# Sample preparation inside the last projection tiles: memory values four requests at a time, rows spread by transfers, retention state updated without TensorE

## The chip, the cores and the metric

One core of one Trainium2 chip. TensorE multiplies (PE; its weight loads are PEld), VectorE is DVE, ScalarE is ACT, GpSimd is POOL, and SyncE (SP) only issues transfers (DMA). The metric is the time of one execution in microseconds on the device; for a timed kernel the median of several runs. All arithmetic is float32 or its TensorE form fp32r.

## The reference

One step of a decoder layer, for a prompt of 2048 tokens and for 8 sample requests of one token each. Every row is normalised and multiplied by one input projection; then three branches run side by side: retention (a recurrent state of 128x128 in each of 4 heads), latent attention over a paged cache of 16384 tokens per request, and cross attention over 256 memory keys and values. What this change touches is the sample side of retention and memory attention, and the head norm of the prompt's retention:

```python
def step(S, inp):                                   # retention, one chunk (a sample has one token)
    qb, kb, vb = inp
    sc = jnp.einsum('bihd,bjhd->bhij', qb, kb) * intra[None]
    o = (jnp.einsum('bhij,bjhe->bihe', sc, vb)
         + jnp.einsum('bihd,bhde->bihe', qb * q_dec[None, :, :, None], S))
    S = S * s_dec[None, :, None, None] + jnp.einsum('bjhd,bjhe->bhde', kb * k_dec[None, :, :, None], vb)
    return S, o

def head_norm(o, g):
    mu = jnp.mean(of, axis=-1, keepdims=True)
    var = jnp.mean((of - mu) ** 2, axis=-1, keepdims=True)
    y = ((of - mu) * lax.rsqrt(var + EPS)).reshape(B, T, H * dv)
    return (y * g.astype(jnp.float32)).astype(o.dtype)

def mem_attend(q, mk, mv):
    s = jnp.einsum('bthd,bmhd->bhtm', q, mk).astype(jnp.float32) * MEM_SCALE
    p = jax.nn.softmax(s, axis=-1).astype(mv.dtype)
    return jnp.einsum('bhtm,bmhd->bthd', p, mv).reshape(B, T, MEM_W)
```

## The kernel before

The kernel runs in stages, each in a block of its own with a barrier behind it. Two of them matter here.

**The projection** (up to about 917 us). The weight columns are cut into stripes, a stripe into tiles. A tile of the last stripes is 24 matmuls of 128x512 (`tile`, L675), into one of two banks of `pj_ps`: even tiles are read out by ACT (L473), odd ones by DVE (L571), and tile n can begin when tile n-2 has been read out. SP stores each pair of tiles to `s_zt` (L381). DVE and ACT also split each stripe's weights into high and low parts (L456, L539), and POOL loads the next stripe (L306). The last 24 tiles carry a second program, `SamplePrepare`: behind tile k each engine runs its own method with that k (`sample.tensor(k)`, `sample.vector(k)`, `sample.scalar(k)`, `sample.sync(k)`; POOL has four parts j = 0 to 3, the last beginning after its last weight load). I call what stands behind tile k "step k". Each engine goes through tiles and steps in program order, so a wait in a step also holds the tiles behind it on that engine. What the steps compute that the change touches:

- `spread(b)` (L2867), steps 4 to 11: one matmul each, which copies the memory query of request b to all 128 partitions; DVE multiplies the request's keys with it and sums (`memory_scores`, L2669 and L2672).
- `key_of(b)` on ACT and `outer(b)` on PE (L2856), steps 7, 8, 11, 12: the outer product of key and value of request b, four matmuls; DVE adds it to the decayed state (`new_state`, L2660). The state of four requests is loaded at a time (`load_state`), multiplied with the retention query (`retention`, L2875) and stored (`store_state`, POOL, j = 3).
- `memory_values(b)` (L2887), steps 14 to 21: eight matmuls of 128x32 weights with 128 columns, all of one request and so all into the same 32 partitions of the bank; two buffers for the loads of the values.
- the transposes of `w_uk` (L2911) and of the page table (L2914) in step 1.

**The sample attention with the prompt's retention** (about 922 to 1477 us). 64 steps g. POOL gathers a group of pages into one of four buffers, after the step that used the buffer is through (`pv_ps`); DVE turns it in three pieces (L2038), PE multiplies with it (L2262, L2275, L2286). Between these steps one block of 128 prompt rows is begun every four: its retention ends in step 4b+4 with `new_state`, `head_statistics` and `head_roots` on DVE, then `normalise` on ACT and `turn_retention` on PE. `head_roots` is `inverse_root` (L102 to L107, eleven small instructions in a chain) and one more (L2101).

Of the kernel before, what the change touches and what calls it, by code (L numbers as in the profile page):

```python
# [28 lines left out]
P = 128  # L29
# [1844 lines left out]
def sample_attention_and_retention(nc, t, keep):  # L1874
# [7 lines left out]
    with ExitStack() as ctx:  # L1882
# [49 lines left out]
        tmp = m.sb("tmp", [P, HEADS])  # L1932
# [14 lines left out]
         bias_ok, exp_ok_m, scT_ok, inv_ok, pn_ok, state_ok, root_ok, pT_ok, cat_m_ok, normed_ok, cat_r_ok, state_out) = [  # L1947
            m.sem(n) for n in ("consts qT_ps kT_ps mem_ps st_ps sc_ps out_ps pT_ps pv_ps rT_ps qT_ok kT_ok "
                               "bias_ok exp_ok scT_ok inv_ok pn_ok state_ok root_ok pT_ok cat_m_ok normed_ok cat_r_ok "
# [12 lines left out]
        with nc.Block() as block:  # L1962
# [48 lines left out]
            @block.gpsimd  # L2011
            def _(pool):
                for g in range(1, STEPS):
                    if g == 3:
                        pool.wait_ge(z_in[0], 32)
                    if g >= DEEP:
                        pool.wait_ge(pv_ps, g - DEEP + 1)
                    gather(pool, t, index, g, nat[g % DEEP], kp[g % DEEP], nat_in[g % DEEP])

            @block.vector  # L2020
            def _(dve):
# [66 lines left out]
                def head_statistics(b):  # L2088
                    for h in range(HEADS):
# [5 lines left out]
                    link(dve.tensor_scalar(var[:, :], mean_var[:, :, 1], EPS, None, ALU.add))  # L2095

                def head_roots(b):
                    if b >= 1:
                        dve.wait_ge(normed_ok, b)
                    inverse_root(dve, link, var[:, :], root[:, :], tmp[:, :])  # L2100
                    dve.scalar_tensor_tensor(shift[:, :], mean_var[:, :, 0], -1.0, root[:, :], ALU.mult, ALU.mult)\  # L2101
                       .then_inc(root_ok, 1)

                for g in range(STEPS + 2):
# [19 lines left out]
                    if begun(g, 3) is not None:  # L2124
                        head_roots(begun(g, 3))
# [310 lines left out]
class SamplePrepare:  # L2436


    def __init__(self, nc, t, ctx, r, keep, rows4, out_rows, banks, turned_over, banks_free, rows_out, gates_out):
        def sb(name, shape, dt=F32):  # L2440
# [8 lines left out]
        self.mem = ring[:, :].rearrange("p (j m n) -> p j m n", j=2, m=MT)  # L2449
# [36 lines left out]
        self.k_only = self.zq[:, 0:2 * W3].rearrange("b (j n) -> b j n", j=2)  # L2486
# [20 lines left out]
        (self.z_in, self.zq_in, self.rot_in, self.ident_in, self.small, self.pick_in, self.uq_in, self.uk_in, self.row_in, self.st_in,  # L2507
         self.zeros, self.chain, self.cqn_ok, self.kv_ok, self.qk_ok, self.q_ok, self.prod_ok, self.low_ok, self.st_ok, self.rg_ok,
         self.kq_ok, self.sm_ok, self.bias_ok, self.pm_ok, self.cq_ps, self.uk_ps, self.uq_ps, self.new_ps, self.qT_ps, self.ql_ps,
         self.qlT_ps, self.rq_ps, self.low_ps, self.outer_ps, self.ret_ps, self.retT_ps, self.rt_ps, self.rgT_ps, self.bc_ps,  # L2510
         self.smT_ps, self.pmT_ps, self.mo_ps, self.moT_ps, self.cqT_ok, self.ukT_ok, self.newT_ok, self.qnT_ok, self.ql_ok, self.q4_ok,
         self.rq_ok, self.ko_ok, self.rows_ok, self.ret_ok, self.exp_ok, self.pmp_ok, self.cats_ok, self.pages_in, self.pages_ok,
         self.index_ps, self.q_clear, self.queries_in, self.q32_ok, self.ret_out, self.out) = [r.sem("s_" + n) for n in (
            "z_in zq_in rot_in ident_in small pick_in uq_in uk_in row_in st_in "
            "zeros chain cqn_ok kv_ok qk_ok q_ok prod_ok low_ok st_ok rg_ok "
            "kq_ok sm_ok bias_ok pm_ok cq_ps uk_ps uq_ps new_ps qT_ps ql_ps "
            "qlT_ps rq_ps low_ps outer_ps ret_ps retT_ps rt_ps rgT_ps bc_ps "
            "smT_ps pmT_ps mo_ps moT_ps cqT_ok ukT_ok newT_ok qnT_ok ql_ok q4_ok "
            "rq_ok ko_ok rows_ok ret_ok exp_ok pmp_ok cats_ok pages_in pages_ok "
            "index_ps q_clear queries_in q32_ok ret_out out").split()]  # L2520
        self.mem_in = [r.sem(f"s_mem_in{j}") for j in range(2)]
# [6 lines left out]
    def sync(self, k, sp):  # L2528
        t, keep = self.t, self.keep

        def load_memory(name, b):
            sp.dma_start(self.mem[:, b % 2, :, :], self.memory_of(name, b)).then_inc(self.mem_in[b % 2], 16)
# [6 lines left out]
        if k == -1:  # L2539
# [14 lines left out]
            sp.dma_start(self.zq[:, :], t["s_zs"][:, 0:3 * W3]).then_inc(self.zq_in, 16)  # L2554
            sp.dma_start(self.zm[:, :], t["s_zs"][:, O_MQ:O_GATE]).then_inc(self.zq_in, 16)
# [15 lines left out]
        if k == 2:  # L2571
            sp.wait_ge(self.uq_ps, 1)
            load_state(0)
        if 4 <= k <= 9:
            sp.wait_ge(self.kq_ok, k - 3)
            load_memory("cache_mem_k", k - 2)
# [7 lines left out]
        if k == 9:  # L2584
# [3 lines left out]
        if k == 10:  # L2588
            sp.wait_ge(self.kq_ok, 7)
            load_memory("cache_mem_v", 0)  # L2590
        if k == 11:
            sp.wait_ge(self.kq_ok, 8)
            load_memory("cache_mem_v", 1)
        if 14 <= k <= 19:
            sp.wait_ge(self.mo_ps, k - 13)
            load_memory("cache_mem_v", k - 12)
# [40 lines left out]
    def vector(self, k, dve):  # L2637
# [17 lines left out]
        def new_state(b):  # L2655
            if b % HALF == 0:
                dve.wait_ge(self.st_in, 16 * (b // HALF + 1))
            dve.wait_ge(self.outer_ps, b + 1)
            for h in range(HEADS):
                last = dve.scalar_tensor_tensor(self.state[:, b % HALF, h, :], self.state[:, b % HALF, h, :], self.decay[h],  # L2660
                                                (A, B)[b % 2][:, h * HD:(h + 1) * HD], ALU.mult, ALU.add)
            last.then_inc(self.st_ok, 1)

        def memory_scores(b):
            if b == 0:
                dve.wait_ge(self.ql_ps, 1)
            dve.wait_ge(self.mem_in[b % 2], 16 * (b // 2 + 1))
            dve.wait_ge(self.bc_ps, b + 1)
# [410 lines left out]
```

## Time and profile before

| | |
|---|---|
| median of 3 runs | 2280.73 us (2277.04 to 2282.85) |
| the profiled execution's own time | 2287.12 us |
| its span, first to last instruction | 2285.4 us |
| PE busy, share of the span | 2135.5 us, 93% |
| DVE busy | 1293.5 us, 57% |
| ACT busy | 666.0 us, 29% |
| POOL busy | 230.3 us, 10% |
| granted TensorE clock, mean | 0.973 |

The profiled execution took 6.4 us more than the median of the timed runs, so differences are taken within the profile and then applied to the median. The times in the rows are microseconds from the start of the span. Busy shares say little by themselves: in each stage one has to see which engine waits, and what its wait ends on.

### The profile page before, as it was taken

The numbers are of one execution on the slowest core, as the hardware profiler recorded it, in microseconds if no ns is written. First come the engines' busy times: TensorE is split into PE (matmuls) and PEld (weight loads), VectorE is DVE, ScalarE is ACT, GpSimd is POOL, SyncE is SP. The second block draws the span as 40 slices with busy tenths as digits, with TensorE's granted clock in tenths as the row PEclk, the third lists the DMA queues.
The fourth block names the chain that finished last, engine by engine and source line by source line (L and its number), as shares of the span: only waits on it lengthen the run. The fifth ranks groups of instructions, "written<-read, shape, count | busy, mean of one in ns | idle before, by whom it ended". The sixth has DMA issues, their size and how long they took to land. (4 is left out here: it accounts for less than half of the span.)

```text
span 2285.4 us, 48464 instructions
## 1 busy us (share of the span) xinstructions
PE 2135.5 (93%) x20401; PEld 1791.2 (78%) x20401; DVE 1293.5 (57%) x2743; ACT 666.0 (29%) x1484; POOL 230.3 (10%) x295
## 2 busy tenths in 40 slices
PE   7999999999999999698999989869899999989998
PEld 6999999997777778476777767648788888768886
DVE  4412444111122431699899999767577777745555
ACT  5311222000111110143343333334345445521110
POOL 1000000000001000121222222011212110000000
PEclk9999999999999999799999999969999999999999
DMA  7322332211224542899999999488997282154542
GB/s 255 112 76 78 100 100 93 84 57 65 84 84 149 190 141 84 326 370 347 338 379 368 362 363 377 180 269 302 345 200 141 53 141 98 58 185 138 163 158 83
DMA packets 186972, 428.19 MB, mean 187 GB/s; under 512 B 15424, under 2 KB 104672, under 8 KB 178576
## 3 DMA queue, kind: packets, MB, share of 16 engines
q0 software_dynamic: 46640, 240.85, 32.2%
q1 hardware_dynamic: 140128, 184.41, 24.3%
q8 instruction: 154, 2.52, 0.4%
q14 instruction: 50, 0.41, 0.1%
HBM read 331.72 MB, written 93.30 MB: 186 GB/s over the span
## 5 line engine op out<-in xcount | busy, mean ns | idle before, releaser
L678 PE MATMUL pj_ps<-pj_wh,pj_xh 128*128 128x256 f32 (+1 forms) x1152 | 324.7, 282 | 2.8 <-issue 2.8
L678 PE MATMUL pj_ps<-pj_wh,pj_xl 128*128 128x256 f32 (+1 forms) x1152 | 322.2, 280 | 0.0
L678 PE MATMUL pj_ps<-pj_wl,pj_xh 128*128 128x256 f32 (+1 forms) x1152 | 322.1, 280 | 0.0
L571 DVE TENSOR_SCALAR pj_stage<-pj_ps 128x256 f32<-128x256 f32 (+2 forms) x72 | 38.5, 535 | 449.4 <-PE pj_ps L675 282.3
L678 PEld LDWEIGHTS pj_ps<-pj_wh,pj_xh 128*128 128x128 f32 x1152 | 218.7, 190 | 10.6 <-issue 10.1
L2038 DVE STREAM_TRANSPOSE sa_turned<-sa_nat 128x2048 f32<-128x2048 f32 x96 | 220.0, 2291 | 10.4 <-DMA sa_kp<-cache_kpe,keep_index 10.4
L2262 PE MATMUL sa_ps_s<-sa_turned,keep_q 128*32 128x128 f32 x5120 | 183.1, 278 | 38.4 <-DVE sa_turned L2038 34.6
L678 PEld LDWEIGHTS pj_ps<-pj_wl,pj_xh 128*128 128x128 f32 x1152 | 218.8, 190 | 0.0
L678 PEld LDWEIGHTS pj_ps<-pj_wh,pj_xl 128*128 128x128 f32 x1152 | 218.7, 190 | 0.0
L675 PE MATMUL pj_ps<-pj_xh,pj_wh 128*128 128x512 f32 x512 | 208.2, 407 | 0.0
L675 PE MATMUL pj_ps<-pj_xl,pj_wh 128*128 128x512 f32 x512 | 204.1, 399 | 0.0
L675 PE MATMUL pj_ps<-pj_xh,pj_wl 128*128 128x512 f32 x512 | 203.6, 398 | 0.0
L2262 PEld LDWEIGHTS sa_ps_s<-sa_turned,keep_q 128*32 128x32 f32 x5120 | 135.2, 111 | 64.7 <-DVE sa_turned L2038 43.0
L473 ACT ACTIVATE pj_stage<-pj_ps 128x256 f32<-128x256 f32 (+2 forms) x72 | 34.1, 473 | 426.4 <-PE pj_ps L675 249.2
L1429 DVE TENSOR_TENSOR la_pl<-la_ps_p,la_ph 128x512 fp32r<-128x512 f32 (+1 forms) x144 | 88.4, 656 | 72.0 <-ACT la_ph L1475 72.0
L675 PEld LDWEIGHTS pj_ps<-pj_xh,pj_wh 128*128 128x128 f32 x512 | 97.9, 191 | 33.8 <-issue 12.4
L675 PEld LDWEIGHTS pj_ps<-pj_xl,pj_wh 128*128 128x128 f32 x512 | 97.6, 191 | 22.6
L675 PEld LDWEIGHTS pj_ps<-pj_xh,pj_wl 128*128 128x128 f32 x512 | 98.2, 192 | 21.2
L1466 ACT ACTIVATE la_row<-la_row,la_soft 128x128 f32<-128x128 f32 (+7 forms) x64 | 77.2, 1206 | 128.2 <-DVE la_soft L1416 128.2
L2286 PE MATMUL sa_ps_o<-sa_nat,sa_p_turned 128*16 128x256 f32 x1536 | 97.5, 385 | 9.8 <-issue 9.7
L1408 DVE CUSTOM_DVE_ANT_0 la_row<-la_ps_s,begin_causal 128x512 f32<-128x512 f32 (+3 forms) x160 | 92.2, 605 | 9.9 <-PE la_ps_s L1532 9.9
L1475 ACT CAST la_ph<-la_ps_p 128x512 fp32r<-128x512 f32 (+1 forms) x144 | 74.4, 565 | 39.3 <-PE la_ps_p L1545 38.4
(455 smaller groups left out, 4324.8 us busy)
## 6 DMA issues: line engine op xcount, KB each, us to landing
pj_raw<-w_in POOLq DMA_DIRECT2D x22, 1024.0 KB, 6.1
s_zn<-pj_stage SPq DMA_DIRECT2D x64, 256.0 KB, 2.2
s_zt<-pj_stage SPq DMA_DIRECT2D x32, 512.0 KB, 2.7
rm_z<-s_zn SPq DMA_DIRECT2D x16, 768.0 KB
pn_x<-x_prompt SPq DMA_DIRECT2D x16, 512.0 KB, 3.7
s_k<-lp_st SPq DMA_DIRECT2D x16, 512.0 KB, 8.8
s_v<-lp_st SPq DMA_DIRECT2D x32, 256.0 KB, 4.6
s_qn<-lp_st SPq DMA_DIRECT2D x16, 512.0 KB, 5.4
```

Source lines behind the costliest of these rows:

```text
L473: act.activation(stage_view(n, w_tile), ps[:, bank_of(n), 0:w_tile], ACT.Copy, scale=factor(s)).then_inc(ev_act, 1)
L571: dve.tensor_scalar(stage_view(n, w_tile), ps[:, bank_of(n), 0:w_tile], factor(s), None, ALU.mult).then_inc(ev_dve, 1)
L675: mm = pe.matmul(ps[:, bank_of(n), :], wt[:, k, m * P:(m + 1) * P], of[c // 2][:, k, c % 2 * 512:(c % 2 + 1) * 512], **flags)
L678: mm = pe.matmul(ps[:, bank_of(n), 0:w], of[u // 8][:, k, u % 8 * P:(u % 8 + 1) * P], wt[:, k, 0:w], **flags)
L1408: dve.tensor_tensor_reduce(out=row[:, s, q, c * P:(c + w) * P], in0=ps_s[:, (at + n) % 3, 0:w * P], in1=m, scale=1.0, scalar=-3.0e38, op0= ...
L1429: dve.tensor_tensor(pl[:, n % RING, 0:w], ps_p[:, n % RING, 0:w], ph[:, n % RING, 0:w], ALU.subtract).then_inc(pl_ok, 1)
L1466: act.activation(row[:, s, q, 0:n], row[:, s, q, 0:n], ACT.Exp, bias=soft[:, s, q, 1:2], scale=MLA_SCALE, accum_out=soft[:, s, q, 2:3]).th ...
L1475: act.copy(ph[:, n % RING, 0:w], ps_p[:, n % RING, 0:w]).then_inc(ph_ok, 1)
L2038: dve.transpose(turned[:, s, a:z, :, :].rearrange("p c x q -> p x c q"), of.rearrange("p x (c q) -> p x c q", q=QR)).then_inc(t_ok, 1)
L2262: mm = pe.matmul(ps_s[j * QR:(j + 1) * QR, s, 0:TQ * QR], q32[:, u, c, :], turned[:, s, c, j * TQ:(j + 1) * TQ, :].rearrange("p x q -> p ( ...
L2286: mm = pe.matmul(ps_o[j * QR:j * QR + ROWS_Q, 0:KVL], p_turned[:, s, x, j, :], nat[g % DEEP][:, TQ * j + x, :], start=(x == 0), stop=(x == ...
```

## The change

What it does, part by part:

- **Memory queries** are copied to 128 partitions by a transfer for each request (`query_row`, in `load_keys`) in place of `spread`.
- **State**: ACT multiplies the loaded state of four requests by the decay (`fade_state`, steps 4 and 9); `new_state` takes the key as a column of scalars from four more small transposes in step 3 (`keys`), and the value from a row copied to 128 partitions by a transfer (`value_row`, loaded in steps -1, 5, 6 and 10). `key_of` and `outer` are gone. `new_state` moves to steps 5, 6, 10, 11, `retention` to steps 7 and 12.
- **Memory values**: four value buffers (two in `ring`, two in the place of the state), `memory_values(i)` for four requests in steps 15 and 18, the requests in the innermost loop.
- **Order**: the transposes of `w_uk` and pages go from step 1 to step 2, behind the products with `w_uq`; the steps behind follow.
- **Head roots** of the prompt's retention go from DVE to POOL, by a power.

```diff
+                def head_roots(b):
+                    pool.wait_ge(power_ok, 1 + 2 * b)
+                    pool.wait_ge(var_ok, b + 1)
+                    if b >= 1:
+                        pool.wait_ge(normed_ok, b)
+                    pool.tensor_tensor(root[:, :], var[:, :], half[:, :], ALU.pow).then_inc(power_ok, 1)
+                    pool.tensor_scalar(negative[:, :], mean_var[:, :, 0], -1.0, 1.0, ALU.mult, ALU.mult).then_inc(power_ok, 1)
+                    pool.wait_ge(power_ok, 2 * b + 3)
+                    pool.tensor_tensor(shift[:, :], negative[:, :], root[:, :], ALU.mult).then_inc(root_ok, 1)
...
+                    if begun(g - 2, 3) is not None:
+                        head_roots(begun(g - 2, 3))
...
-                def head_roots(b):
-                    if b >= 1:
-                        dve.wait_ge(normed_ok, b)
-                    inverse_root(dve, link, var[:, :], root[:, :], tmp[:, :])
-                    dve.scalar_tensor_tensor(shift[:, :], mean_var[:, :, 0], -1.0, root[:, :], ALU.mult, ALU.mult)\
-                       .then_inc(root_ok, 1)
...
+        def load_keys(b):
+            sp.dma_start(self.query_row[:, b % 2, :], t["s_zs"][b:b + 1, O_MQ:O_GATE].to_broadcast([P, W3])).then_inc(self.key_in[b % 2], 16)
+            sp.dma_start(self.mem[b % 2], self.memory_of("cache_mem_k", b)).then_inc(self.key_in[b % 2], 16)
+        def load_value_row(b):
+            sp.dma_start(self.value_row[:, b % 2, :], t["s_zs"][b:b + 1, O_RV:O_CQ].to_broadcast([P, W3])).then_inc(self.row_in[b % 2], 16)
...
+        if k in (5, 6, 10):
+            n = {5: 2, 6: 4, 10: 6}[k]
+            sp.wait_ge(self.st_ok, n)
+            load_value_row(n)
+            load_value_row(n + 1)
-        if k == 9:
+        if k == 8:
             sp.wait_ge(self.ret_ps, 1)
             sp.wait_ge(self.ret_out, 16)
             load_state(1)
...
         def new_state(b):
-            if b % HALF == 0:
-                dve.wait_ge(self.st_in, 16 * (b // HALF + 1))
-            dve.wait_ge(self.outer_ps, b + 1)
+            dve.wait_ge(self.faded_ok, b // HALF + 1)
+            dve.wait_ge(self.rq_ok, 1)
+            dve.wait_ge(self.row_in[b % 2], 16 * (b // 2 + 1))
             for h in range(HEADS):
-                last = dve.scalar_tensor_tensor(self.state[:, b % HALF, h, :], self.state[:, b % HALF, h, :], self.decay[h],
-                                                (A, B)[b % 2][:, h * HD:(h + 1) * HD], ALU.mult, ALU.add)
+                last = dve.scalar_tensor_tensor(self.state[:, b % HALF, h, :], self.value_row[:, b % 2, h * HD:(h + 1) * HD],
+                                                self.keys[:, h, b:b + 1], self.state[:, b % HALF, h, :], ALU.mult, ALU.add)
...
+        def fade_state(i):
+            act.wait_ge(self.st_in, 16 * (i + 1))
+            for h in range(HEADS):
+                last = act.activation(self.state[:, :, h, :], self.state[:, :, h, :], ACT.Copy, scale=self.decay[h])
+            last.then_inc(self.faded_ok, 1)
...
-        def memory_values(b):
-            if b == 0:
-                pe.wait_ge(self.pmp_ok, 1)
-                pe.wait_ge(self.st_ok, DEC)
-            pe.wait_ge(self.mem_in[b % 2], 16 * (DEC // 2 + b // 2 + 1))
-            j = b % HALF
+        def memory_values(i):
+            pe.wait_ge(self.pmp_ok, 1)
+            pe.wait_ge(self.rq_ok, 1)
+            pe.wait_ge(self.value_in, 16 * HALF * (i + 1))
             for h in range(HEADS):
                 for m in range(MT):
-                    mm = pe.matmul((A, B)[b // HALF][32 * j:32 * j + 32, h * HD:(h + 1) * HD], self.pm_pad[:, m, b * HEADS + h, :],
-                                   self.mem[:, b % 2, m, h * HD:(h + 1) * HD], start=(m == 0), stop=(m == MT - 1))
+                    for j in range(HALF):
+                        mm = pe.matmul((A, B)[i][32 * j:32 * j + 32, h * HD:(h + 1) * HD], self.pm_pad[:, m, (HALF * i + j) * HEADS + h, :],
+                                       self.mem[j][:, m, h * HD:(h + 1) * HD], start=(m == 0), stop=(m == MT - 1))
```

On SP's queue before the change, steps 4 to 8: the keys of a request (`sp_ring<-cache_mem_k`), the tile stores, and the 16 small transfers of step 5 that rearrange the queries.

```order
 L2532 DMA sp_ring<-cache_mem_k 128x2x512
 L381 DMA s_zt<-pj_stage 128x1024
 L2532 DMA sp_ring<-cache_mem_k 128x2x512
 L2582 DMA sp_queries<-sp_q 32x3x32 x16
 L2532 DMA sp_ring<-cache_mem_k 128x2x512
 L381 DMA s_zt<-pj_stage 128x1024
```

The same place after it:

```order
 L381 DMA s_zt<-pj_stage 128x1024
 L2544 DMA sp_query_row<-s_zs 128x512
 L2545 DMA sp_ring<-cache_mem_k 128x2x512
 L2602 DMA sp_queries<-sp_q 32x3x32 x16
 L2551 DMA sp_value_row<-s_zs 128x512 x2
 L2544 DMA sp_query_row<-s_zs 128x512
 L2545 DMA sp_ring<-cache_mem_k 128x2x512
 L2551 DMA sp_value_row<-s_zs 128x512 x2
 L381 DMA s_zt<-pj_stage 128x1024
```

The value rows of requests 2 and 3 now stand directly behind the 16 transfers of step 5, those of requests 4 and 5 in step 6.

On PE, the steps 7 to 9 before the change (the tiles' matmuls left out): `spread`, the sum for the new row (L2953), `outer`, `retention`.

```order
 L2867 MATMUL pj_ps_t<-sp_zm,sp_one_row 128x512
 L2953 MATMUL pj_ps_row4<-sp_psum,sp_first 128x8 x4
 L2856 MATMUL pj_ps<-sp_zq 128x128 x8
...
 L2867 MATMUL pj_ps_t<-sp_zm,sp_one_row 128x512
 L2856 MATMUL pj_ps<-sp_zq 128x128 x8
...
 L2867 MATMUL pj_ps_t<-sp_zm,sp_one_row 128x512
 L2875 MATMUL pj_ps_row<-sp_weights,sp_rq_pad 32x128 x16
```

After it, step 7 has the sum and `retention` (L2873) of the first four requests, and steps 8 to 11 nothing:

```order
 L2948 MATMUL pj_ps_row4<-sp_psum,sp_first 128x8 x4
 L2873 MATMUL pj_ps_row<-sp_weights,sp_rq_pad 32x128 x16
```

`retention` has moved two tiles forward, and the states of requests 2 and 3 must be ready by then.

## Rows read from the trace of the kernel before

**Rows 1.** Windows, sample stage: us, busy PE, PEld, DVE, ACT, POOL, PEclk, DMA share, GB/s

```profile
1115.00:1445.00 330.00, 304.04 (x6532) 236.52 (x6522) 313.94 (x562) 125.67 (x410) 75.02 (x80) 1.00 0.96 367
```

**Rows 2.** Groups of instructions on PE, 690 to 945 us

```profile
L2887 PE MATMUL pj_ps<-sp_ring,sp_turns 128*32 128x128 f32 x128 | 15.5, 274 | 0.0
...
L2867 PE MATMUL pj_ps_t<-sp_zm,sp_one_row 8*128 8x512 f32 x16 | 9.0, 640 | 0.0
L2856 PE MATMUL pj_ps<-sp_zq 8*128 8x128 f32 x64 | 8.3, 278 | 0.0
L2875 PE MATMUL pj_ps_row<-sp_weights,sp_rq_pad 128*32 128x128 f32 x64 | 2.2, 276 | 0.0
```

**Rows 3.** Timeline of PE, last projection tiles: start us, us, what, [idle before]

```profile
740.25 1.97 PE L2911 MATMUL pj_ps_t<-keep_ident,sp_ring 128*128 128x128 f32 x8 [2.34 <-DMA sp_ring<-w_uk]
744.19 0.27 PE L2914 MATMUL pj_ps_row<-keep_ident,sp_pages_f 64*16 64x64 f32 x1 [1.97 <-DVE sp_pages_f L2689]
744.39 0.79 PE L675 MATMUL pj_ps<-pj_xh,pj_wh 128*128 128x512 f32 x1
...
752.70 1.18 PE L2920 MATMUL pj_ps_row<-sp_weights,sp_cqT 128*32 128x192 f32 x24
...
767.82 0.50 PE L675 MATMUL pj_ps<-pj_xh,pj_wh 128*128 128x512 f32 x1
...
773.42 0.38 PE L2944 MATMUL pj_ps<-keep_ident,sp_angle 128*128 128x128 f32 x2
...
791.37 0.79 PE L675 MATMUL pj_ps<-pj_xh,pj_wh 128*128 128x512 f32 x1
...
798.51 0.69 PE L2867 MATMUL pj_ps_t<-sp_zm,sp_one_row 8*128 8x512 f32 x1
```

**Rows 4.** Window, columns as in rows 1: the tile behind step 1's waits

```profile
744.40:750.00 5.60, 5.60 (x14) 4.44 (x14) 4.50 (x8) 0.00 (x0) 0.00 (x0) 0.50 0.76 230
```

**Rows 5.** Timeline of SP's queue, step 5

```profile
776.69 10.54 SPq L2582 DMA_DIRECT2D sp_queries<-sp_q  x16
```

**Rows 6.** Transfers: count, KB each, us from issue to landing

```profile
sp_ring<-cache_mem_k SPq DMA_DIRECT2D x8, 512.0 KB, 5.4
...
new_ret_s<-sp_weights POOLq DMA_DIRECT2D x2, 1024.0 KB, 6.1
...
sp_queries<-sp_q SPq DMA_DIRECT2D x16, 12.0 KB, 2.3
```

**Rows 7.** Timeline of DVE, step 8

```profile
801.00 1.22 DVE L2672 TENSOR_REDUCE sp_sm<-sp_rows 128x8 f32<-128x1024 f32 x1
802.25 1.67 DVE L2660 SCALAR_TENSOR_TENSOR sp_weights<-sp_weights,pj_ps 128x128 f32<-128x128 f32 x8
```

**Rows 8.** Timeline of DVE, sample stage, end of a block

```profile
1111.63 0.17 DVE L2095 TENSOR_SCALAR rm_var<-rm_mean_var 128x4 f32<-128x4 f32 x1
...
1113.00 0.13 DVE L102 TENSOR_SCALAR rm_tmp<-rm_var 128x4 int32<-128x4 int32 x1
...
1115.22 2.31 DVE L2038 STREAM_TRANSPOSE sa_turned<-sa_nat 128x2048 f32<-128x2048 f32 x1
```

**Rows 9.** Timeline of PE, two waits of a block, sample stage

```profile
1120.05 1.08 PE L2262 MATMUL sa_ps_s<-sa_turned,keep_q 128*32 128x128 f32 x32 [0.67 <-DVE sa_turned L2038]
...
1145.57 0.65 PE L2262 MATMUL sa_ps_s<-sa_turned,keep_q 128*32 128x128 f32 x16 [0.75 <-DVE sa_turned L2038]
```

**Rows 10.** Waits, 1115 to 1445 us: total us, times, longest

```profile
PE sa_ps_s L2262 <- DVE sa_turned L2038: 13.6, 18, 1.2
...
DVE sa_turned L2038 <- DMA keep_kp<-cache_kpe,keep_index: 2.0, 3, 1.1
```

**Rows 11.** Window with the highest DMA rate, columns as in rows 1

```profile
940.00:960.00 20.00, 14.72 (x291) 11.04 (x284) 12.81 (x15) 4.68 (x18) 1.88 (x2) 0.80 1.01 404
```

**Rows 12.** Timeline of POOL: a power in the first stage, a gather's issue

```profile
7.19 0.73 POOL L291 TENSOR_TENSOR pn_stat<-pn_stat,pn_half 128x2 f32<-128x2 f32 x1
...
1115.81 0.94 POOL L1868 DMA_INDIRECT sa_nat<-cache_ckv,keep_index  x1 [7.47 <-PE sa_ps_o L2286]
```

More of the change, by code:

```diff
@@ L2012, in _ @@
             def _(pool):
-                for g in range(1, STEPS):
+                def head_roots(b):
[7 more added lines that the diff above has]
+                    pool.tensor_tensor(shift[:, :], negative[:, :], root[:, :], ALU.mult).then_inc(root_ok, 1)
+                pool.memset(half[:, :], -0.5).then_inc(power_ok, 1)
+                for g in range(1, STEPS + DEEP):
                     if g == 3:
                         pool.wait_ge(z_in[0], 32)
-                    if g >= DEEP:
-                        pool.wait_ge(pv_ps, g - DEEP + 1)
-                    gather(pool, t, index, g, nat[g % DEEP], kp[g % DEEP], nat_in[g % DEEP])
+                    if g < STEPS:
+                        if g >= DEEP:
+                            pool.wait_ge(pv_ps, g - DEEP + 1)
+                        gather(pool, t, index, g, nat[g % DEEP], kp[g % DEEP], nat_in[g % DEEP])
+                    if begun(g - 2, 3) is not None:
+                        head_roots(begun(g - 2, 3))
             @block.vector
@@ L2448, in __init__ @@
         ring = sb("ring", [P, 2 * MT * W3])
-        self.mem = ring[:, :].rearrange("p (j m n) -> p j m n", j=2, m=MT)
+        self.mem = [of[:, j * MT * W3:(j + 1) * MT * W3].rearrange("p (m n) -> p m n", m=MT) for of in (ring, weights) for j in range(2)]
         self.w_uk = ring[:, 0:2 * W3].rearrange("p (c h d) -> p c h d", c=2, h=HEADS)
@@ L2520, in __init__ @@
             "index_ps q_clear queries_in q32_ok ret_out out").split()]
-        self.mem_in = [r.sem(f"s_mem_in{j}") for j in range(2)]
+        self.key_in = [r.sem(f"s_key_in{j}") for j in range(2)]
+        self.row_in = [r.sem(f"s_row_in{j}") for j in range(2)]
+        self.value_in = r.sem("s_value_in")
         self.decay = [float(1.0 - 2.0 ** (-5.0 - h)) for h in range(HEADS)]
@@ L2587, in sync @@
             load_state(1)
-        if k == 10:
-            sp.wait_ge(self.kq_ok, 7)
-            load_memory("cache_mem_v", 0)
         if k == 11:
             sp.wait_ge(self.kq_ok, 8)
[L2593 to L2596, printed above, removed]
+            load_values(0)
+            load_values(1)
+        if k == 12:
+            sp.wait_ge(self.ret_ps, 2)
+            sp.wait_ge(self.ret_out, 32)
+            load_values(2)
+            load_values(3)
+        if k == 15:
+            sp.wait_ge(self.mo_ps, 1)
+            for b in range(HALF, DEC):
+                load_values(b)
     def pool(self, j, pool):
@@ L2922, in tensor @@
             mm.then_inc(self.uq_ps, 1)
-            pe.wait_ge(self.pages_ok, 2)
-            pe.matmul(E[:, P:P + STEPS], self.steps[:, :], self.pagesT[:, :], start=True, stop=True).then_inc(self.index_ps, 1)
+            pe.wait_ge(self.uk_in, 16)
+            for c in range(2):
+                for h in range(HEADS):
+                    mm = pe.transpose((C, D_)[c][:, h * P:(h + 1) * P], self.w_uk[:, c, h, :], ident[:, :])
+            mm.then_inc(self.uk_ps, 1)
+            pe.wait_ge(self.pages_ok, 1)
+            pe.transpose(E[0:GP, 0:STEPS], self.pages_f[:, :], ident[0:STEPS, 0:STEPS]).then_inc(self.index_ps, 1)
         if k == 3:
@@ L2930, in tensor @@
             pe.wait_ge(self.newT_ok, 1)
-            for h in range(HEADS):
+            for h in range(2 * HEADS):
                 mm = pe.transpose(B[:, h * DEC:(h + 1) * DEC], self.qk[:, h, :], small_id)
             mm.then_inc(self.rq_ps, 1)
+            pe.wait_ge(self.pages_ok, 2)
+            pe.matmul(E[:, P:P + STEPS], self.steps[:, :], self.pagesT[:, :], start=True, stop=True).then_inc(self.index_ps, 1)
         if k == 4:
@@ L2969, in tensor @@
             mm.then_inc(self.smT_ps, 1)
-            outer(6)
-            outer(7)
+            retention(1)
         if k == 13:
@@ L2976, in tensor @@
             mm.then_inc(self.pmT_ps, 1)
-            retention(1)
         if k == 14:
```

153 lines of the change are left out of this document (52 added, 101 removed).

## The prediction

> **What bounds the kernel now.** I read the table of the page first, then the windows, to see which engine is full where, then for each of the two touched places the timeline of the full engine and the waits.
>
> In the last 24 projection tiles PE is never without work except at one place. A tile takes 5.60 us at full clock (767.82 to 773.42) [rows 3], and whatever stands between two tiles is added to the path in full: DVE, ACT and SP wait for PE there, not PE for them. The exception is step 1: PE waits 2.34 us for `w_uk` and 1.97 us for the page table [rows 3], and the tile behind runs at a granted clock of 0.50, that is 1.2 GHz [rows 4]. That tile takes 8.31 us (744.39 to 752.70). The tile behind the first `outer` pair takes 7.14 us (791.37 to 798.51), for the same reason: the clock fell for part of it [rows 3]; the timeline has three such tiles, each behind outer products.
>
> In the sample stage three things are nearly full at once: DVE 313.94 us of 330, PE 304.04, the DMA engines 0.96 of their time [rows 1]. PE is the tightest in dependence: it goes from step to step without a gap, but waits on DVE twice a block of four steps, 0.67 and 0.75 us [rows 9], 13.6 us in the 330 [rows 10]. The 0.67 follows directly on `head_roots`; the 0.75 stands where DVE itself had to wait for PE's `retention_values`, a loop that the change leaves alone.
>
> **The change part by part.** Projection tiles, all of it on PE's path:
>
> - `outer`: 8.3 us busy in 64 rows; `spread`: 9.0 in 16 [rows 2]. Neighbouring matmuls overlap by about 0.07 us (L2914 is busy for 0.27, the next starts 0.20 behind it [rows 3]), twelve groups, so 8.0 + 8.3 = 16.3 gone.
> - `memory_values`: 128 rows take 15.5 us, 0.12 each. `retention` has the same shape, 128x32 weights and 128 columns, with the requests (that is, the 32-partition strips of the output) innermost, and takes 2.2 us for 64 rows, 0.034 each [rows 2]. The new order is `retention`'s. 128 x 0.034 = 4.4; less the overlaps the part falls from 14.9 to 4.1: 10.8 gained. Bounds: 0 (as now) and 10.8.
> - Step 1: without `w_uk` and pages in it both waits go, 4.3 us; both inputs are there by 744.19, and in step 2 PE comes to them at about 744.6 (the first wait began at 740.25 - 2.34 = 737.9; a tile 5.6, the products with `w_uq` 1.1 [rows 3]). The slow tile goes back to full clock, 8.31 - 5.60 = 2.7, and the eight transposes, 1.97 us at half clock [rows 3], take 1.0 less. With `outer` gone I take the three slow tiles as gone too, 3 x 1.5 = 4.5. Together 12.5.
> - Added: four more tiny transposes, 0.3.
>
> That is 39.3 gained. Now what the moves cost. `retention(0)` in step 7 needs the states of requests 0 to 3; requests 2 and 3 need value rows that SP issues behind the 16 query transfers. Counted from PE's end of step 5: DVE reads out tile 5 and multiplies request 1's keys, 1.9 us, which releases SP's key loads, 0.8; the 16 transfers take 10.5 [rows 5]; the row's issue 0.4, its landing at least 2.3 (12 KB) and at most 5.4 (512 KB under load) [rows 6]; I take 3 for 256 KB; two requests of `new_state`, 1.67 us [rows 7]. Sum 18.3 (17.6 to 20.7). PE needs two tiles and the sum matmuls, 2 x 5.65 + 1.0 = 12.3. So PE waits 6.0 us (5.3 to 8.4) in step 7, longer than in step 1 today, and I charge the same slow tile behind it, 2.6. Behind the waiting DVE stand its read-out of tile 7 and the keys of request 3; behind SP the tile stores. All have a tile's slack.
>
> Second chain: `store_state(0)` (6.1 us [rows 6]) begins when POOL's last weight load is out, about two tiles into the stripe; then `load_state(1)` in step 8, ACT's `fade_state` in step 9 (four passes over 512 elements, about 2.4), `new_state` of 4 and 5, the rows for 6 and 7, `new_state` again. I get st_ok at 8 within 1 us of PE's arrival in step 12; charge 1 (0 to 10). If the state lands late ACT stands in step 9 and cannot read out tile 10, which stops PE at tile 12. DVE's key product now reads two SBUF operands instead of PSUM; its 1.22 us are hidden. ACT's fading replaces `key_of`, hidden. Extra transfers, 16 of 256 KB = 4 MB in 150 us, are hidden.
>
> Net for the tiles: 39.3 - 6.0 - 2.6 - 1.0 = 29.7.
>
> Sample stage: DVE loses `head_roots`, 1113.00 to 1115.22 = 2.2 us per block [rows 8]. PE was late by only 0.67 for it [rows 9], afterwards it is full itself; so 0.67 x 15 = 10.0, and 1.5 us of DVE's 2.2 turn into its idle time. In the last block nothing follows but the final fold, which waits for DVE: the whole 2.2. Sum 12.2. Bounds: 0 if the transfers hold the stage, 35 if PE's gaplessness is only how its ends are drawn. POOL's part: a power on 2 columns takes 0.73 us [rows 12]; with 4 columns and two small operations I estimate 1.5. The variance is ready at 1111.8 [rows 8], POOL's next gather is released at 1115.81 [rows 12]: it fits with 2.5 us to spare, and `normalise` starts earlier than now.
>
> 29.7 + 12.2 = 41.9. The profiled execution took 2287.1 us, so 2245 in a profile; on the median of 2280.7: **2239 us**.
>
> One rule is to be weighed. The window of the highest rate shows 404 GB/s at a DMA share of 1.01 [rows 11], the stage runs at 367 and 0.96 [rows 1]; its 330 us are ten blocks of 33.0, and a block of 32.3 needs 375. By the rows there is room, and DVE waited only 2.0 us for the pages [rows 10]. The Trainium skill, page "SBUF — State Buffer", section "A bandwidth-pool intuition that's wrong (but worth ruling out)", gives about 358 GB/s from HBM to one core. By that figure the stage would be at its end already and gain only its last 2.2 us. The trace's 404 disagrees, though in a short piece.
>
> **The rivals.**
>
> A. *No stall in step 7.* The row lands fast and PE arrives later than I count. For it: any slow tile ahead delays PE. Against: 10.5 us of issue are in a row of the trace. 39.3 + 12.2 = 51.5: 2229.
>
> B. *The transfers hold the sample stage.* DVE leads by 1.5 us more and runs into the gathers: the share is 0.96, and a rate at 1.00 share would be 367 / 0.96 = 382, only 4% more. Against: the 404 [rows 11]. Then 29.7 + 2.2 = 32: 2249. This is also where the Trainium skill's figure above would lead.
>
> C. *The state chain is late.* Store, load, fade, rows stand one behind another over two queues; each 5 us of lateness costs 5 and a slow tile, 2.6. With 8 us in sum 10 to 11 more lost: 2250. The same time if the interleaved values do not overlap (10.8 less): 2250.
>
> D. *Slower: POOL holds the gathers.* Now POOL waits for DVE inside the gather loop. From the variance to the next release there are 4.0 us. If POOL's three operations took more, each gather behind them would be late, and with the DMA at 0.96 no block could make it up. 0.3% slower means losing 41.9 + 6.9 = 49, 3.3 us in each of 15 blocks: POOL would need 7.3 us. At 8 us: 15 x 4.0 = 60 lost, 2299. Against it: 0.73 us for a power.
> The Trainium skill, page "SBUF — State Buffer", section "SBUF: two separate sides", says that a GpSimd operation and a VectorE operation with two SBUF inputs block each other for a whole instruction; by it the power could wait for one DVE instruction. No run yet shows it for this place.
>
> **How the numbers follow.** Forecast 0.40 (own range 2231 to 2246), A 0.15, B 0.20, C 0.20, D 0.03, the rest 0.02 for no gain. The range leaves out D and half of the outer parts of A and C: 2223 to 2261. Faster by over 0.3% (6.9 us, about what a measurement of this kernel can tell): 0.94, the same 0.03, slower 0.03.
>
> **What the next profile would show.** The last tile ends some 30 us earlier than now, near 887. No waits of PE in step 1 and a full-clock tile behind; in step 7 a wait of 5 to 8 us before `retention`, ended by DVE's `new_state`, itself waiting for `sp_value_row`; 32 interleaved value matmuls (64 rows) in 2.0 us; no slow tiles in steps 8 to 12. In the sample stage the 0.67 us waits gone, DVE's idle up by 1.5 us a block, blocks of 32.3 us. Wrong would make me: PE waiting in steps 10 to 12, value matmuls at 0.12 us each, `sa_turned` waiting for gathers block by block, or gaps before POOL's gathers.

## The result, and the profile after

| | before | after |
|---|---|---|
| median | 2280.58 us (4 runs) | 2251.47 us (4 runs, 2248.19 to 2260.78) |
| ratio | | 0.988, 95% interval 0.9848 to 0.9913 |
| the profiled execution, its span | 2287.12, 2285.4 us | 2248.19, 2246.4 us |
| PE busy, share of the span | 2135.5 us, 93% | 2094.4 us, 93% |
| DVE / ACT / POOL busy | 1293.5 / 666.0 / 230.3 us | 1266.8 / 666.5 / 255.3 us |
| granted TensorE clock, mean | 0.973 | 0.978 |

The change makes the kernel 29 us faster; 2239 was forecast, in a range of 2223 to 2261. I read it in two parts. From the first transposes of step 1 to the end of the last tile it was 179.3 us and is 154.4: 24.9 gained of 29.7 forecast. The rest of the median's gain, some 4 us, stands against the 12.2 forecast for the sample stage.

The 29 us lie inside the stated range, but outside the forecast's own one (2231 to 2246). The nearest sums are those of the rivals B (2249) and C (2250); what became of the two is told below.

PE, last projection tiles (start us, us, what, [idle before]), beside [rows 3]:

```profile
743.39 1.18 PE L2910 MATMUL pj_ps_row<-sp_weights,sp_cqT 128*32 128x192 f32 x24
744.50 1.09 PE L2916 MATMUL pj_ps_t<-keep_ident,sp_ring 128*128 128x128 f32 x8
745.53 0.22 PE L2919 MATMUL pj_ps_row<-keep_ident,sp_pages_f 64*16 64x64 f32 x1
...
776.16 1.03 PE L2948 MATMUL pj_ps_row<-sp_psum,sp_first 128*128 128x8 f32 x8 [0.49 <-issue]
785.69 1.93 PE L2873 MATMUL pj_ps_row<-sp_weights,sp_rq_pad 128*32 128x128 f32 x32 [8.49 <-DVE sp_weights L2689]
...
812.86 0.47 PE L675 MATMUL pj_ps<-pj_xh,pj_wh 128*128 128x512 f32 x1 [1.38 <-ACT pj_stage L473]
...
820.55 0.39 PE L2954 MATMUL pj_ps_t<-keep_ident,sp_sm 128*32 128x128 f32 x2 [1.97 <-DVEq L2769]
821.55 1.93 PE L2873 MATMUL pj_ps_row<-sp_weights,sp_rq_pad 128*32 128x128 f32 x32 [0.61 <-DVE sp_weights L2689]
```

Step 2 has no waits now: what step 1 waited 4.3 us for is there. In their place PE waits 8.49 us in step 7, and in steps 11 and 12 three times, 1.38, 1.97 and 0.61. Both groups of `retention` take 1.93 us instead of 1.08: the granted clock was 0.50 behind both waits.

DVE ahead of the wait in step 7, and SP's queue:

```profile
782.29 1.14 DVE L2689 SCALAR_TENSOR_TENSOR sp_weights<-sp_value_row,sp_keys,sp_weights 128x128 f32<-128x128 f32 x4 [6.22 <-DMA sp_value_row<-s_zs]
784.50 1.14 DVE L2689 SCALAR_TENSOR_TENSOR sp_weights<-sp_value_row,sp_keys,sp_weights 128x128 f32<-128x128 f32 x4 [1.07 <-DMA sp_value_row<-s_zs]
```

```profile
767.42 10.71 SPq L2602 DMA_DIRECT2D sp_queries<-sp_q  x16
778.17 1.06 SPq L2551 DMA_DIRECT2D sp_value_row<-s_zs  x2
...
803.55 0.79 SPq L2554 DMA_DIRECT2D sp_weights<-state_ret  x1
```

The chain is the one forecast: 16 transfers are issued in 10.71 us, the rows behind them, and DVE waits for the rows.

Transfers, 690 to 900 us (count, KB each, us to landing), beside [rows 6]:

```profile
sp_ring<-cache_mem_k SPq DMA_DIRECT2D x8, 512.0 KB, 7.3
sp_value_row<-s_zs SPq DMA_DIRECT2D x8, 256.0 KB, 5.4
...
new_ret_s<-sp_weights POOLq DMA_DIRECT2D x2, 1024.0 KB, 8.9
```

Keys and store take longer than before (5.4 and 6.1 us). The 8.9 is the middle of two: the first store took 11.0, the second 6.9.

The memory values, one of the two groups of 32 matmuls, 64 rows of the profile (window, columns as in [rows 1]):

```profile
841.81:843.70 1.89, 1.89 (x66) 1.69 (x65) 0.69 (x1) 1.73 (x1) 0.00 (x0) 1.00 0.06 26
```

The sample stage: its window, the waits of DVE and of PE from 900 and 925 us on (total, times, longest), and POOL at the end of a block:

```profile
1090.00:1420.00 330.00, 304.26 (x6478) 236.83 (x6469) 293.76 (x438) 126.03 (x407) 90.72 (x110) 0.99 0.95 362
```

```profile
DVE sa_turned L2055 <- DMA sa_kp<-cache_kpe,keep_index: 30.0, 21, 7.8
...
PE sa_ps_o L2296 <- issue: 14.7, 9, 2.7
PE sa_ps_s L2272 <- DVE sa_turned L2055: 10.4, 16, 0.9
```

```profile
1214.40 1.05 POOL L2021 TENSOR_TENSOR rm_root<-rm_var,rm_half 128x4 f32<-128x4 f32 x1 [2.40 <-issue]
1215.45 0.19 POOL L2022 TENSOR_SCALAR rm_negative<-rm_mean_var 128x4 f32<-128x4 f32 x1
1215.72 0.20 POOL L2024 TENSOR_TENSOR rm_shift<-rm_negative,rm_root 128x4 f32<-128x4 f32 x1
1218.15 1.06 POOL L1868 DMA_INDIRECT sa_nat<-cache_ckv,keep_index  x1 [2.23 <-PE sa_ps_o L2296]
```

DVE is busy 20 us less than in [rows 1], PE as long as then, 304 of 330: the time that DVE no longer spends isn't seen in PE's work per us. DVE waits more for the pages, 30.0 us in all. POOL's three operations take 1.52 us and end 2.2 us ahead of the next gather's release; in all 15 blocks that have such a gather they are through 2.2 us or more ahead of it. POOL holds nothing.

### The profile page after: what moved, and what is told of

Its sections match the earlier page's. It is cut to its first block and busy times, and to the rows that moved or that the text cites. A ratio compares the mean times of both kernels' runs of the same rounds, so it can differ in the third digit from the quotient of the medians.

```text
span 2246.4 us, 48190 instructions
## 1 busy us (share of the span) xinstructions
PE 2094.4 (93%) x20325; PEld 1763.6 (79%) x20325; DVE 1266.8 (56%) x2551; ACT 666.5 (30%) x1485; POOL 255.3 (11%) x344
## 3 DMA queue, kind: packets, MB, share of 16 engines
q1 hardware_dynamic: 142400, 188.54, 25.1%
## 5 line engine op out<-in xcount | busy, mean ns | idle before, releaser
L678 PEld LDWEIGHTS pj_ps<-pj_wh,pj_xh 128*128 128x128 f32 x1152 | 218.8, 190 | 10.6 <-issue 10.1
L2296 PE MATMUL sa_ps_o<-sa_nat,sa_p_turned 128*16 128x256 f32 x1536 | 98.2, 384 | 12.4 <-issue 12.3
L306 POOL DMA_DIRECT2D pj_raw<-w_in x23 | 20.6, 896 | 640.9 <-PE pj_ps_row L691 606.9
```

The lines of the kernel that those rows point to most:

```text
L306: pool.dma_start(raw[:, s % 2, :, 0:w], w_rows[:, :, c0:c0 + w]).then_inc(w_in[s % 2], 16)
L678: mm = pe.matmul(ps[:, bank_of(n), 0:w], of[u // 8][:, k, u % 8 * P:(u % 8 + 1) * P], wt[:, k, 0:w], **flags)
L2296: mm = pe.matmul(ps_o[j * QR:j * QR + ROWS_Q, 0:KVL], p_turned[:, s, x, j, :], nat[g % DEEP][:, TQ * j + x, :], start=(x == 0), stop=(x == ...
```

## The experiments

### The two parts alone

`roots_only` is the kernel before with `head_roots` on POOL; `roots_back` is the changed kernel with it on DVE:

```diff
-                    if begun(g - 2, 3) is not None:
-                        head_roots(begun(g - 2, 3))
...
+                    if begun(g, 3) is not None:
+                        head_roots(begun(g, 3))
```

> The kernel before with one part of the change: the head roots on POOL. Theory 1 (DVE is what PE waits for in the sample stage): PE's waits of 0.67 us per block and the 2.2 us at the end go, 12 us faster than before, about 2268. Theory 2 (the gathers are the limit as soon as DVE leads): 2 us faster, and the number of steps in which DVE waits for pages rises well above the 7 of the kernel before.

> The changed kernel with the head roots back on DVE, so the projection's part alone. By theory 1 it is 12 us slower than the changed kernel, about 2264 (17 us faster than before); by theory 2 only 2 us slower, about 2253. PE's waits in the steps 7 and 12 of the projection stay as they are in the changed kernel: 8.5 and 2.6 us.

`roots_only`: 2276.69 us, ratio 0.9975 (0.9958 to 0.9993), 5.0 us faster than before. `roots_back`: 2260.52, 0.9894 (0.9872 to 0.9916). The changed kernel, timed again as `again`, has 2251.45 and 0.9887 (0.9869 to 0.9905):

> The changed kernel itself once more, as the measure for the others of this call. It was 2251.5 us in four runs, 29 us faster than before; the same is expected, 2247 to 2256.

So the head roots are worth 5 us by the first pair, whose interval (1.6 to 9.6) leaves out the 12 of theory 1 but not the 2 of theory 2; the other pair gives 9 by its medians and 2 by its ratios. Most of PE's waits for DVE in the sample stage did go as forecast. The first row of PE's waits is from `roots_back`; the two below it are from `roots_only`, and the first of them holds 8.9 us of the stage's start:

```profile
PE sa_ps_s L2262 <- DVE sa_turned L2038: 19.0, 27, 1.0
```

```profile
PE sa_ps_s L2272 <- DVE sa_turned L2055: 25.1, 19, 8.9
...
PE sa_ps_o L2296 <- issue: 11.6, 8, 2.1
```

19.0 against 25.1 - 8.9 = 16.2 would be little; without the first step of the stage (from 20 us behind its start) it is 19.0 against 10.2, in the changed kernel 10.4, and in nine profiles with the roots on POOL 11.3 on the mean. 8 us of waits are gone where 10.0 were forecast (over the whole stage 34.8, the mean of `before` and `roots_back`, against 28.3, the mean of the nine: 6.5).

### Do the gathers hold the sample stage?

`light_before` and `light_after` gather the 4 KB rows for 64 of 128 partitions only, from step 8 on (the rest of the buffer keeps old values):

```diff
+    part = slice(0, P if g < 8 else P // 2)
-    pool.indirect_dma_start(out=kp[:, :, :]...
+    pool.indirect_dma_start(out=kp[part, :, :]...
```

> The changed kernel, in which from step 8 of the sample attention the second gather of each step brings only 64 of its 128 partitions (the other half keeps old values): 1.05 MB less of 12.1 MB in a block. Theory 2 (the gathers limit the sample stage now): DVE's waits for pages go, the block falls by 1 to 1.5 us, 13 to 20 us faster than the changed kernel, about 2235. Theory 1 (PE limits it): at most 4 us faster.

> The kernel before with the same lighter gathers. There DVE's row of work limited the blocks: at most 5 us faster than before, by both theories; were it 13 us or more, the gathers limited the stage before the change too, and taking work from DVE could never give 12 us.

Both missed, in the other direction: `light_before` took 2286.89 us (1.004, 1.0023 to 1.0057), 8 us more than before, and `light_after` 2265.98 (0.994, 0.9917 to 0.9963), 15 more than the changed kernel. The window of `light_after`:

```profile
1090.00:1420.00 330.00, 292.74 (x6225) 222.14 (x6224) 284.25 (x417) 121.23 (x394) 84.19 (x103) 0.98 0.93 325
```

Fewer bytes, 325 GB/s, and still a DMA share of 0.93: each packet takes longer, in the records of 1100 to 1400 us 217 ns against 161 for one of 4 KB. Half the partitions is not half the load. (Where `light_before` lost its 8 us its profile doesn't show: from the last tile to the last product of the stage it took 571.6 us, before 572.1.) The Trainium skill, page "SBUF — State Buffer", section "Door 1: The DMA port swizzle (why `[64,N]` ≈ `[32,N]`)", says that bandwidth depends on how many of the 16 ports the partitions reach, and by its formula the first 64 reach eight. The packet times agree; the ports themselves no run here shows. The pair does not answer the question. `even_after` does: it brings a quarter of each row, to all 128 partitions (of other tokens than the reference's).

```diff
+    less = 1 if g < 8 else 4
-    pool.indirect_dma_start(out=kp[:, :, :].rearrange("p t c -> p (t c)"), ...
+    pool.indirect_dma_start(out=kp[:, :, :].rearrange("p t c -> p (t c)")[:, 0:TPP * ROPE // less], ...
```

> The changed kernel, in which from step 8 of the sample attention the second gather of each step brings 1 KB for each partition instead of 4 KB (a quarter of the row, of other tokens), on all 128 partitions: 1.5 MB less of 12.1 MB in a block. If the gathers limit the sample stage after the change, DVE's waits for pages (30 us in the stage) fall below 10 and it is 10 to 20 us faster than the changed kernel. If PE alone limits it, the gain is under 4 us. PE's gaps that end 1.4 us behind the landing of a code fetch should become fewer if full DMA engines are what makes these fetches late.

Result: 2249.76, 0.9878 (0.9859 to 0.9896), 1.7 us faster than `again` beside it, which is no difference. Its window and DVE's waits for pages:

```profile
1090.00:1420.00 330.00, 306.09 (x6541) 236.48 (x6544) 295.57 (x441) 126.71 (x410) 91.27 (x110) 0.98 0.87 318
```

```profile
DVE sa_turned L2056 <- DMA sa_kp<-cache_kpe,keep_index: 10.1, 3, 7.8
```

The DMA share fell from 0.95 to 0.87 and DVE's waits for pages from 24.8 (`again`) to 10.1, and nothing was gained: the gathers do not hold the stage. Rival B falls. One block of the changed kernel (1214 to 1245 us) took 31.0 us and moved 388 GB/s. The Trainium skill, page "SBUF — State Buffer", section "A bandwidth-pool intuition that's wrong (but worth ruling out)", gives about 358 GB/s from HBM to one core; the 388 disagree.

What does stand in PE's way are gaps that the profile can only call "issue". The longest, and the transfers of the same 3 us:

```profile
1379.47 1.90 PE L2296 MATMUL sa_ps_o<-sa_nat,sa_p_turned 128*16 128x256 f32 x26 [2.70 <-issue]
```

```profile
q8 instruction: 1, 0.02, 1.9%
```

The transfer carries a piece of PE's program: the records of this queue (q8) show pieces of 16 KB alone, one for 264 of PE's matmuls and weight loads in the first 200 us, one for 264 from 1000 to 1200 and one for 245 from 1200 to 1450. This piece moved from 1377.14 to 1378.08, and PE goes on 1.4 us behind its landing. All 10 gaps of 0.9 us or more in the changed kernel's stage (16.2 us in all) end 1.2 to 1.5 us behind the landing of such a piece, and the 5 of before (10.5 us) 1.3 to 1.6. With the roots on DVE I count 10.5 (before) and 7.9 us (`roots_back`), in the nine profiles with them on POOL and full gathers 11.6 to 25.6, mean 18.5. That would be where half of the forecast gain went: time that PE had spent waiting for DVE became time waiting for its program. It isn't shown: `light_before`, with the roots on DVE, has 20.7.

A gap can cost more than its length, since the granted clock can fall behind it. In `late_fade`:

```profile
1230.59 0.61 PE L2296 MATMUL sa_ps_o<-sa_nat,sa_p_turned 128*16 128x256 f32 x4 [2.94 <-issue]
```

```profile
1231.70:1235.10 3.40, 3.40 (x66) 3.04 (x68) 2.33 (x4) 0.00 (x0) 1.66 (x2) 0.50 0.69 190
```

PE stood for 2.94 us, and from 1231.70 on the clock was 0.50, that is 1.2 GHz, for 3.4 us, in which PE was busy throughout; I estimate that half of it, 1.7 us, is lost. All 32 half-clock stretches that the 14 profiles show between the stage's first 60 us and its last product begin in or within 1.5 us behind such a gap; five are in `late_fade`, two in `before` (10.2 us), none in `roots_back`. Those two have the same code in this stage and took 572.1 and 563.3 us from the last tile to the last product: 2.6 of the 8.8 are gaps, and by my estimate 5.1 (half of 10.2) are the clock.

What makes a piece late stays open. `even_after`, with a mean DMA share of 0.87, still has 19.1 us of gaps, so a lower mean didn't help; but in all 14 profiles the engines were fuller just ahead of the late pieces. Of 898 pieces that began to move behind 2 us at a share of 0.90 or more, PE waited for 147; of the 222 others for 10. No run changes that alone.

### Step 7

`rows4` has four value rows, two of them in the place of `zq`, which is free from step 2 on. The rows of requests 2 and 3 go there, ahead of the 16 query transfers:

```diff
         if k == 2:
...
+            sp.wait_ge(self.qk_ok, 1)
+            load_value_row(2)
+            load_value_row(3)
...
-        if k in (5, 6, 10):
-            n = {5: 2, 6: 4, 10: 6}[k]
+        if k in (6, 7):
+            n = {6: 2, 7: 4}[k]
             sp.wait_ge(self.st_ok, n)
-            load_value_row(n)
-            load_value_row(n + 1)
+            load_value_row(n + 2)
+            load_value_row(n + 3)
```

> The changed kernel with four buffers for value rows: those of requests 2 and 3 are loaded in step 2, ahead of the 16 query transfers. If these transfers are what makes step 7 late, PE's wait of 8.5 us, the retention at half clock (0.9) and the slow tile behind it (2.7) go: 12 us faster than the changed kernel, about 2239, and up to 5 more if step 12's lateness comes from the rows as well. Rival: DVE or the fading of the state is as late as the rows; then PE still waits 5 us or more in step 7 and the gain is under 5 us.

2246.3 us, 0.9836 (0.9812 to 0.986): against the changed kernel 5 us less by the medians and 10 to 12 by the ratios, whose intervals are too wide to tell these from each other or from the 12 expected. The trace can: tiles and steps take 148.6 us instead of 154.4. PE:

```profile
779.70 1.08 PE L2878 MATMUL pj_ps_row<-sp_weights,sp_rq_pad 128*32 128x128 f32 x32 [1.02 <-DVE sp_weights L2694]
...
809.82 0.77 PE L675 MATMUL pj_ps<-pj_xh,pj_wh 128*128 128x512 f32 x1 [6.45 <-ACT pj_stage L473]
```

The 16 transfers were the cause: 8.49 is down to 1.02, and `retention` runs at full clock. Step 7 and the tile behind it take 9.6 us less. But 3.8 of these are paid back: four tiles later PE's wait grew from 1.38 to 6.45, and the tile behind it takes 8.30 us; some of that comes back in step 12, where PE no longer waits. ACT's read-out of tile 10 stands behind its fading, the fading waits for the next states, these for the store of the first:

```profile
786.47 1.21 POOL L2637 DMA_DIRECT2D new_ret_s<-sp_weights  x1
```

```profile
800.66 0.79 SPq L2556 DMA_DIRECT2D sp_weights<-state_ret  x1
```

14.1 us for a store that took 6.1 before.

### What makes the states late

`store_early` moves the first store to SP, behind the `st_ok` wait of step 7; `fewer_rows` leaves out the query rows of requests 2 to 7; `late_fade` moves the second fading behind ACT's read-out of tile 10, the four `new_state` behind it to step 11 and the retention to step 13. All three start from `rows4`:

```diff
             sp.wait_ge(self.st_ok, n)
+            if n == HALF:
+                sp.dma_start(t["new_ret_s"]... [:, 0:HALF * HEADS, :], ...).then_inc(self.ret_early, 16)
...
+            if b < 2:
+                sp.dma_start(self.query_row[:, b % 2, :], ...
...
-        if k in (4, 9):
+        if k in (4, 10):
             fade_state(0 if k == 4 else 1)
```

> The kernel with four value rows, and the first store of states moved from POOL, where it stands behind the last stripe's weight load, to SP in step 7, as soon as the states are there. In the kernel with four value rows the store is issued at 786.5 and its completion lets the load of the next states start at 800.7, 14 us later, and PE waits 6.45 us for tile 10's read-out, which stands behind ACT's fading. If the store's place behind the 1 MB weight load is the cause, the store is through 8 us or more earlier, the 6.45 us and the slow tile behind (2.6) go: 9 us faster than with four value rows, about 2237. Rival: the state's load itself or SP's queue is late; then PE still waits over 3 us there and the gain is under 4 us.

> The kernel with four value rows, without the query rows of requests 2 to 7 (their scores use the rows of requests 0 and 1): six transfers of 256 KB less. If the store and the load of the states are slow (14.1 and 6.3 us) because the added rows fill the DMA engines, the store takes 11 us or less and PE's wait of 6.45 us for tile 10's read-out falls below 3. Rival: the store is slow for its place behind the 1 MB weight load alone; then it stays at 13 to 14 us and the wait at 5 to 7.

> The kernel with four value rows, in which ACT fades the second four states behind tile 10's read-out instead of ahead of it, DVE updates all four in step 11, and the retention of them stands in step 13. If PE's wait of 6.45 us is only due to ACT's read-out standing behind the fading, it goes, and with it the slow tile (2.7): 9 us faster than with four value rows, about 2237. Rival: the lateness moves on; DVE now waits for the fading ahead of tile 11's read-out or in step 11, and PE waits as long one or two tiles later: gain under 3 us.

| | median us | ratio (95%) | tiles us | store us | PE's wait us |
|---|---|---|---|---|---|
| `rows4` | 2246.3 | 0.9836 (0.9812 to 0.986) | 148.6 | 14.1 | 6.45 |
| `store_early` | 2242.35 | 0.9842 (0.9816 to 0.9869) | 146.6 | 13.2 | 3.69 |
| `fewer_rows` | 2243.52 | 0.985 (0.9832 to 0.9869) | 146.5 | 13.4 | 6.04 |
| `late_fade` | 2246.9 | 0.9851 (0.9829 to 0.9872) | 146.5 | 14.0 | 4.75 |

Each gains some 2 us in the tiles and nothing that the ratios can tell. Neither the place behind the weight load in POOL's queue nor the query rows make the store slow: it takes over 13 us without either. In `late_fade` the lateness moved on, as its rival said: SP's queue stood at the store too, and the keys of the last request came late, so that DVE and behind it PE (`L2961`) waited:

```profile
813.20 0.61 PE L2961 MATMUL pj_ps_t<-keep_ident,sp_sm 128*32 128x128 f32 x2 [4.75 <-DVEq L2774]
```

```profile
810.61 1.23 DVE L2702 TENSOR_TENSOR sp_rows<-sp_ring,sp_query_row 128x1024 f32<-128x1024 f32 x1 [6.79 <-DMA sp_ring<-cache_mem_k]
```

What differs from before is what else is under way. There the store was issued at 804.22, 7.6 us behind the last stripe's weight load, and landed after 6.1 us. The two windows from issue to landing, before and in `rows4`:

```profile
804.22:810.35 6.13, 6.13 (x45) 4.23 (x47) 1.15 (x2) 0.00 (x0) 1.20 (x1) 0.97 0.60 175
```

```profile
786.47:800.53 14.06, 14.06 (x62) 11.33 (x61) 7.15 (x14) 0.60 (x1) 1.21 (x2) 1.00 0.90 316
```

Before, 1.08 MB moved in that time, and the store itself is 1.05 of it: it was all but alone. In `rows4` it is issued 0.9 us behind the weight load, and 4.44 MB move until it lands: the weights (11.0 us), keys (12.3), rows and tile stores. In `fewer_rows` it is still 3.96 MB. The 28 stores of the 14 profiles line up: 6.0 to 7.0 us where up to 1.7 MB moved meanwhile, 10.9 to 12.5 with 3.2 to 3.4 MB, 13.2 to 14.1 with 4.0 to 4.7. A longer transfer sees more bytes by itself, so this reading leans on the rate beside it, 316 GB/s against 175. No kernel with the weight load elsewhere was run.

### Memory values and order

```diff
+            for j in range(HALF):
             for h in range(HEADS):
                 for m in range(MT):
-                    for j in range(HALF):
```

> The changed kernel with the requests of the memory values in the outermost loop, so that eight matmuls in a row go to the same 32 partitions again. If the interleaving is what saves, each of the two groups takes 7.4 us instead of 1.89: 11 us slower, about 2262. Rival: the two groups are short because their inputs and weights differ otherwise; then the time stays at 2251.

`values_plain`: 2261.74, 0.9901 (0.988 to 0.9921), 10 us slower than the changed kernel, 7.8 of it in the tiles. Its window of one group:

```profile
842.95:848.83 5.88, 5.88 (x66) 5.68 (x65) 2.98 (x2) 1.90 (x1) 0.00 (x0) 1.00 0.22 89
```

5.88 instead of 1.89 for the same 64 rows. Of the 14.9 - 3.8 = 11.1 us that went, the order of the requests is 8.0; 3.1 come from two groups in the place of eight. The starts show most of it: within one strip of 32 partitions they are 109 ns apart, before and here, but at each change of strip seven of them are only 6 to 103 ns apart, which saves 0.4 us each time.

`order_back` has the transposes of `w_uk` and pages in step 1 again:

```diff
+            pe.wait_ge(self.uk_in, 16)
+            ... (the eight transposes and that of the pages)
         if k == 2:
```

> The changed kernel with the transposes of w_uk and of the page table in step 1 again. By my sum for this part PE waits 4.3 us there, the tile behind runs at half clock (2.7) and the eight transposes as well (1.0): 8 us slower than the changed kernel, about 2259. Rival: the time is made up behind it, since the waits of steps 7 and 12 end on transfers and not on PE; then those waits become shorter by as much, and the difference is under 4 us.

2256.69 us, 0.9891 (0.9866 to 0.9917), 5 us more by the medians; the tiles take 161.6 us, 7.2 more than in the changed kernel, and PE still waits 8.60 us in step 7 (8.49 in the changed kernel), so the rival, time made up there, is out. The two waits are back:

```profile
740.15 1.09 PE L2908 MATMUL pj_ps_t<-keep_ident,sp_ring 128*128 128x128 f32 x8 [1.32 <-DMA sp_ring<-w_uk]
744.34 0.27 PE L2911 MATMUL pj_ps_row<-keep_ident,sp_pages_f 64*16 64x64 f32 x1 [3.10 <-DVE sp_pages_f L2718]
```

## Why the prediction was right, and where its sum was not

- **Outer products, `spread`, values, step 1**: right. Values 11.1 for 10.8; step 1 7.2 (`order_back`) for 8.0; the slow tiles that are left stand behind waits. With the losses below, the gains in the tiles come to 24.9 + 16.6 = 41.5, for 39.3. No run takes the outer products or `spread` out alone: their part (20.5 forecast) is what is left of the sum, 41.5 - 11.1 - 7.2 = 23.2.
- **Step 7**: right in its mechanism, too small in size. "PE waits 6.0 us (5.3 to 8.4)": 8.49, just over the upper bound, and 0.5 ahead of the sum matmuls. The rows landed about 4 us after issue instead of 3, the second one later still, and `new_state` takes 2.28 us instead of the 1.67 that I took from its form with PSUM. `retention` itself at half clock was not in the sum (0.9); the tiles behind lost 1.3, not 2.6. Together 11.2 instead of 8.6.
- **The state chain**: "charge 1 (0 to 10)". It cost 5.4: waits of 4.0 and 1.4 of half clock. This is half of rival C (10 to 11), and one of the signs named for being wrong ("PE waiting in steps 10 to 12") did show. The failed term is "`store_state(0)` (6.1 us)": 11.0. The duration was taken from a place where the store had the engines nearly to itself, and the change moves it beside the weight load. "Extra transfers ... are hidden" failed with it: their bytes are, their effect on the landing of others is not.
- **Sample stage**: the step that failed. "0.67 x 15 = 10.0" held for the waits (8 us gone), "Sum 12.2" did not for the time: `roots_only` gives 5.0 (1.6 to 9.6). Another of the prediction's signs of being wrong, `sa_turned` waiting for gathers, showed too (30.0 us, 21 times), but it costs nothing (`even_after`): rival B came near the time with the wrong reason. PE's gaps behind its program's transfers, and the half clock behind some of them, are the one other candidate the traces show, and that stays open. Rival D is out: 1.52 us for the estimate of 1.5. Nor does the power wait for a DVE instruction, as that rival allowed: all 16 times it begins 0.14 to 0.16 us behind the variance and takes 1.05.
- **From profile to median**: "2245 in a profile; on the median 2239". The profiled time was 2248.19, only 3 off; but before's profile was 6.4 over its median, and this one 3.3 under its own. Of the 39 us between the two profiles 10 are such chance, and I had assumed none; that the 2245 came so near is luck. From the last tile to the last product of the sample stage alone, nine profiles of the same code took between 555.1 and 570.6 us.

The errors of both parts (4.8 in the tiles, some 8 behind them) go the same way, 12.8 in all. The range held because the rivals had widened it, not because the sum was close.

## What to carry to other kernels

A transfer's duration is worth only as much as what is beside it: when a change moves one, count the bytes under way at its new place, and take the duration from a row with as many. When a full engine stops waiting for another, look whether its gaps without a releaser grow, before booking the whole wait as gain. Count the granted clock behind such gaps as well. And matmuls into 32-column strips should go round the strips: 64 rows of them took 1.89 us so and 5.88 strip by strip.

## What was not expected of the hardware

- PE stands still for 0.9 to 3.0 us 5 to 18 times in the sample stage of the 14 profiles, each time until 1.2 to 1.7 us behind the landing of a 16 KB piece of its program; behind some of these gaps the granted clock is 0.50 for 3.4 or 6.8 us.
- A gather of 4 KB rows to the first 64 partitions made both kernels slower than one to all 128, by 8 and 15 us (packets of 217 instead of 161 ns).
- `scalar_tensor_tensor` of 128x128 takes 346 ns with both tensors in SBUF and 280 with one of them in PSUM.
